# Slabs 4 and 5 of the gate/linear product over all units of an item, slabs 6 and 7 unit by unit

## The chip, the cores and the metric

The kernel runs on one core of a Trainium2 chip. The metric is the device time of one execution in microseconds (us), the median of several timed runs. The profile is one further execution recorded by the hardware profiler; its times are in microseconds from the start of the span.

## What is computed

One layer of a transformer with a recurrent group and a spatial gating group, followed by a mixture of experts. Only the last part matters here:

```python
def moe(h, router_w, router_b, w_gu, b_gu, w_down, b_down):
    logits = (hf @ router_w) + router_b              # 1024 tokens, 32 experts
    top_logit, top_e = lax.top_k(logits, TOP_K)      # TOP_K = 4
    ...
    def expert_block(args):
        xb, e = args
        gu = xb @ w_gu[e] + b_gu[e]                  # 1024 -> 2048, f32
        g, lin = jnp.split(gu, 2, axis=-1)
        g = jnp.minimum(g, SWIGLU_LIMIT)
        lin = jnp.clip(lin, -SWIGLU_LIMIT, SWIGLU_LIMIT)
        act = g * jax.nn.sigmoid(SWIGLU_ALPHA * g) * (lin + 1.0)
        return act @ w_down[e] + b_down[e]           # 1024 -> 1024
    ...                                              # times the gate, added per token
```

Everything is in f32. The 4096 assignments of tokens to experts are unevenly spread, so the experts have different numbers of rows.

## The kernel before

**Items and units.** The rows of an expert are cut into units of 32 rows, and up to four units form an item. This input gives 47 items. Item 0 is started by code of its own; the other 46 are worked off by the loop at the end of TensorE's program, `with pe.Fori(0, last_item) as g`. Of these 46, two have one unit, eleven have two, seventeen have three and sixteen have four. An expert with more than four units takes two items one after the other, on the same weights.

**TensorE.** One pass of the loop does `down_of(g)` for item g, that is a small product that makes the list of rows of a later item (`make_list`, L1430), the down product of each unit (`down`, L1499) and another small product (`repeat_rows`, L1442). Then comes `gate_and_linear_of(g + 1)`: the gate/linear product of the next item (L1479). That product is summed over eight slabs of weights, k = 0 to 7. A slab is 1 MB. For one unit and one slab TensorE issues four products of 512 columns, each split in two in the trace (eight records), into the PSUM bank of that unit. I call this a **step**: an item with n units has 8n steps. Slabs 0 to 3 are done slab by slab, each over all units. After a wait on `z_made[1]` slabs 4 to 7 are done unit by unit: four steps of the last unit, then four of the unit before it, down to unit 0. `units_down` runs a body over the units 3, 2, 1, 0, as many as the item has; it is a nest of compare-and-branch instructions (L451). `load_word` (L1463) loads two words of the next item into registers, between the last unit's products.

**Signals.** After the last slab of a unit TensorE raises `gu_made`, for which VectorE waits before it begins that unit's activation. After the product of unit 0 with slab k it raises `freed[k]` (k up to 5), so that the weights of the next expert may overwrite the slab; slabs 6 and 7 are freed in `make_list`, the four chunks of down weights during `down(0)` and `repeat_rows`. Before `down(u)` TensorE waits for `at_made`, the activated and transposed unit u.

**VectorE.** Its loop first prepares later items (L2131, L2119, L1990 to L2006), then runs `activate(u)` for the units in falling order: bias for gate and linear part (L2157, L2159), two clips (L2163, L2165), a wait for ScalarE's sigmoid (L1040), two products (L2168, L2170), and the transpose (L2172), whose end raises `at_made`. After all units come `read_list` and the result of each unit (L2179, L2182). In the last item the activation is followed by the final norm of the eight tiles of the hidden rows (L2281, L2283), into which the last results are mixed.

**Weights.** SyncE's queue issues twelve 1 MB loads for each expert, in the order of the slabs: eight of gate/linear weights (chunks 0 to 7) and four of down weights (8 to 11). Each waits for its own `freed[q]` and is issued behind the ones before it. There is one buffer for each chunk.

Of the kernel before, what the change touches and what calls it, by code (L numbers as in the profile page):

```python
# [176 lines left out]
def build(nc, ins, out):  # L177
# [10 lines left out]
    with ExitStack() as ctx:  # L188
# [260 lines left out]
        def by_units(eng, units, u, body):  # L449

            with eng.If_lt(units, u + 1):  # L451
                eng.nop()
            with eng.Else():
                body()
                eng.nop()

        def units_down(eng, units, body):

            def from_2():
                by_units(eng, units, 3, lambda: body(3))  # L460
                body(2)

            def from_1():
                by_units(eng, units, 2, from_2)
                body(1)

            by_units(eng, units, 1, from_1)
            body(0)
# [25 lines left out]
        def gu_slab(k):  # L494

            at = (k % 2) * 2048
            return big[:, SLOT_OF_PAIR[k // 2], at:at + 2048]
# [611 lines left out]
        def _(pe):  # L1109
# [339 lines left out]
            units = pe.alloc_register("units")  # L1449
# [12 lines left out]
            def load_word(turn, i):  # L1462
                pe.reg_load(loaded[i], items_i[0:1, bass.ds(turn + (IT_PLACE, IT_UNITS)[i] * WORD, 1)])  # L1463
# [7 lines left out]
            def gate_and_linear(u, half, first=False, between=None, steady=False, slabs=None):  # L1471

                for k in slabs or range(4 * half, 4 * half + 4):
                    pe.wait_ge(w_arrived[k], SEMW if first else arrived)
                    rhs = gu_slab(k).rearrange("p (a n) -> p a n", a=2)
                    if k == 0 and u > 0 and steady:
                        pe.wait_ge(dn_drained, results_of[u])
                    for j in range(4):
                        last = pe.matmul(psum[32 * j:32 * j + 32, u, :].rearrange("p (a n) -> p a n", a=2),  # L1479
                                         izT[:, k, u * UNIT:(u + 1) * UNIT], rhs[:, :, 256 * j:256 * j + 256],  # L1480
                                         start=(k == 0), stop=(k == KT - 1), skip_group_check=True)
                    if u == 0 and k < KT - 2 and not first:
                        last.then_inc(freed[k], 1)
                    if between is not None:
                        between(k % 4)
                if half == 1 and not first:
                    last.then_inc(gu_made, 1)
# [92 lines left out]
            def gate_and_linear_of(g):  # L1580

                pe.wait_ge(z_made[0], g + 1)
                for k in range(4):
                    units_down(pe, units, lambda u: gate_and_linear(u, 0, steady=True, slabs=(k,)))
                pe.wait_ge(z_made[1], g + 1)
                units_down(pe, units, lambda u: gate_and_linear(
                    u, 1, between=lambda k: load_word(g + 1, k) if k < 2 and u == 0 else None))

            def down_of(g):

# [4 lines left out]
            with pe.Fori(0, last_item) as g:  # L1595
                down_of(g)
                begin_item()
                results_to_wait_for()
                gate_and_linear_of(g + 1)
# [730 lines left out]
```

## Time and profile before

| | us |
|---|---|
| median of 3 timed runs | 2007.19 (2005.55 to 2008.69) |
| the profiled execution, its own time | 1994.71 |
| its span | 1992.9 |
| TensorE busy | 1921.6 (96%) |
| VectorE busy | 991.6 (50%) |
| mean busy share of the DMA engines' bandwidth | 262 GB/s over the span |

The loop over the items runs from about 465 us to the end. The profile's page groups instructions by line, the timeline gives them in order of time, with the idle time of the engine just before them and what ended it in brackets, and the chain names what the end of the span was waiting for, step by step. TensorE's records of one product appear as two rows of four.

### The profile page before, as it was taken

Reading aid. Unit: us, or ns where it says so; the run is one execution under the profiler, and the core shown is the slowest. Engines: PE = TensorE matmul, PEld = TensorE weight load, DVE = VectorE, ACT = ScalarE, POOL = GpSimd, SP = SyncE. Lnnn points to the kernel's source line nnn. Section 1 sums busy time; section 2 is a strip of 40 time slices with the busy share of each in tenths; the row PEclk is TensorE's granted clock in tenths of the full one; section 3 lists DMA queues with packets and bytes.
Section 4 is the critical chain, followed back from the end, with each engine's and each line's share of the span. In section 5 each row is a group of like instructions: output and inputs, shape, how many; then the busy total and the mean of one; then the engine's idle time right before and its main releaser. Section 6 shows DMA issues by size and latency. Waiting matters only on the chain.

```text
span 1992.9 us, 54916 instructions
## 1 busy us (share of the span) xinstructions
PE 1921.6 (96%) x20484; PEld 805.8 (40%) x20485; DVE 991.6 (50%) x2305; ACT 357.8 (18%) x739; POOL 461.6 (23%) x498
## 2 busy tenths in 40 slices
PE   7999999969899899999999999999999999999996
PEld 4444445424333334343434343333443444344432
DVE  2677565255444444544445444554545454454435
ACT  4353122221111111101111111111111111111003
POOL 1200041033222222122222222222222223222221
PEclk9999999989999999999999999999999999999998
DMA  9433326153843946869595978979889797999985
GB/s 349 162 116 127 127 108 204 69 190 106 338 161 105 350 132 230 338 203 371 173 370 207 386 262 307 384 281 386 292 341 351 279 395 286 389 398 343 328 329 201
DMA packets 120672, 521.86 MB, mean 262 GB/s; under 512 B 14592, under 2 KB 40848, under 8 KB 71472
## 3 DMA queue, kind: packets, MB, share of 16 engines
q1 hardware_dynamic: 88880, 468.41, 60.5%
q0 software_dynamic: 31168, 50.78, 11.0%
q10 hardware_dynamic: 576, 2.10, 0.3%
q8 instruction: 21, 0.34, 0.1%
q14 instruction: 27, 0.22, 0.0%
HBM read 488.85 MB, written 32.78 MB: 262 GB/s over the span
## 4 chain that ended last, share of the span: by engine, by line
PE 91%; DMA 4%; DVE 2%; issue 1%; SPq 1%; DVEq 1%; ACT 0%; POOL 0%; POOLq 0%; ACTq 0%
PE psum L1479 46%; PE psum L1499 24%; PE psum L1153 7%; PE psum L1386 5%; PE psum L1321 3%; DMA big<-in_exp_w_down_dram 3%; PE psum L1220 1%; DMA big<-in_ada_w_dram 1%; PE psum L1254 1%; PE psum L1430 1%; PE psum L1442 0%; DMA big<-in_w_out_dram 0%; PE psum L1314 0%; PE psum L1339 0%; DVEq L444 0%
## 5 line engine op out<-in xcount | busy, mean ns | idle before, releaser
L1479 PE MATMUL psum<-big,r 128*32 128x512 f32 x9152 | 995.8, 594 | 8.2 <-ACT r L1045 4.7
L1479 PEld LDWEIGHTS psum<-big,r 128*32 128x32 f32 x9152 | 292.2, 110 | 665.9 <-issue 656.3
L1499 PE MATMUL psum<-big,r 128*32 128x256 f32 x9152 | 508.7, 382 | 13.0 <-DVE r L2172 9.8
L1499 PEld LDWEIGHTS psum<-big,r 128*32 128x32 f32 x9152 | 295.5, 111 | 205.5 <-DVE r L2172 9.9
L783 POOL DMA_INDIRECT acc_rows<-r,scatter_idx x139 | 221.4, 1593 | 676.3 <-DVE r L2182 617.0
L1030 ACT ACTIVATE r<-r,shift 128x128 f32<-128x128 f32 x368 | 150.9, 481 | 839.5 <-PE psum L1479 798.3
L2179 DVE TENSOR_TENSOR r<-psum,r 128x256 f32<-128x256 f32 x143 | 60.7, 424 | 267.5 <-PE psum L1499 266.5
L2157 DVE TENSOR_TENSOR r<-psum,r 128x256 f32<-128x256 f32 x143 | 60.4, 423 | 251.8 <-PE psum L1479 233.9
L2131 DVE STREAM_TRANSPOSE r<-r 128x1024 f32<-128x1024 f32 x46 | 95.9, 2084 | 170.8 <-issue 170.8
L772 POOL DMA_INDIRECT r<-hs_rows,gather_idx x143 | 142.4, 996 | 123.5 <-issue 123.5
L1040 ACT ACTIVATE r<-r 128x256 f32<-128x256 f32 x143 | 59.6, 417 | 473.9 <-DVE r L2163 473.9
L1153 PE MATMUL psum<-r,big 128*128 128x512 f32 x320 | 139.0, 593 | 0.0
L1386 PE MATMUL psum<-big,r 128*128 128x512 f32 x256 | 112.1, 594 | 1.0 <-DMA big<-in_w_out_dram 1.0
L2172 DVE STREAM_TRANSPOSE r<-r 128x256 f32<-128x256 f32 x143 | 93.6, 654 | 4.9
L1153 PEld LDWEIGHTS psum<-r,big 128*128 128x128 f32 x320 | 60.6, 190 | 75.1 <-issue 75.1
L2168 DVE TENSOR_TENSOR r<-r 128x256 f32<-128x256 f32 x143 | 60.9, 426 | 49.7 <-ACT r L1040 49.7
L762 POOL COPY gather_idx<-r 128x4 int32 (+1 forms) x47 | 8.8, 188 | 316.1 <-DVE r L1999 316.1
L2182 DVE SCALAR_TENSOR_TENSOR r<-r,g1row,g_rows 128x256 f32<-128x256 f32 x143 | 69.3, 485 | 5.1
L1386 PEld LDWEIGHTS psum<-big,r 128*128 128x128 f32 x256 | 47.9, 190 | 59.2 <-issue 57.3
L2119 DVE TENSOR_TENSOR r<-r 128x1024 bf16<-128x1024 f32 (+1 forms) x49 | 60.0, 1225 | 7.1 <-DVE r L2117 1.2
L2170 DVE TENSOR_TENSOR r<-r 128x256 f32<-128x256 f32 x143 | 60.8, 425 | 4.9
L2159 DVE SCALAR_TENSOR_TENSOR r<-psum,r 128x256 f32<-128x256 f32 x143 | 59.2, 414 | 0.1
(326 smaller groups left out, 983.5 us busy)
## 6 DMA issues: line engine op xcount, KB each, us to landing
big<-in_exp_w_gu_dram SPq DMA_DIRECT2D x256, 1024.0 KB, 10.0
big<-in_exp_w_down_dram SPq DMA_DIRECT2D x128, 1024.0 KB, 17.0
big<-in_ada_w_dram SPq DMA_DIRECT2D x8, 2048.0 KB, 13.0
r<-bias_pack SPq DMA_DIRECT2D x128, 96.0 KB
big<-in_ada_w_dram SPq DMA_DIRECT2D x8, 1024.0 KB, 12.6
big<-in_w_in_dram SPq DMA_DIRECT2D x4, 2048.0 KB, 17.3
r<-in_x_dram SPq DMA_DIRECT2D x12, 512.0 KB, 10.2
big<-in_w_out_dram SPq DMA_DIRECT2D x2, 2048.0 KB, 12.8
```

Source lines behind the costliest of these rows:

```text
L772: pool.indirect_dma_start(z_quarters[:, u, :], None, hs_quarters, bass.IndirectOffsetOnAxis(ap=gather_idx[:, u:u + 1], axis=0)).then_inc(r ...
L783: pool.indirect_dma_start(acc_quarters, bass.IndirectOffsetOnAxis(ap=scatter_idx[:, u:u + 1], axis=0), y_sb[:, u, :], None, bounds_check=4 ...
L1030: ins_ = act.activation(izT[:, k, :].rearrange("p (u n) -> p u n", u=UMAX), z_blocks[:, :, k, :], ACT.Identity, bias=shift2[:, 1, k:k + 1] ...
L1153: last = pe.matmul(b, w[:, k, m * P:(m + 1) * P], zT[:, k, th * 512:(th + 1) * 512], start=(k == 0), stop=(k == KT - 1))
L1386: last = pe.matmul(b, src[:, ct % CT, t * P:(t + 1) * P], ring(("wout", dh))[:, ct, :], start=(ct == 0), stop=(ct == 2 * CT - 1))
L1479: last = pe.matmul(psum[32 * j:32 * j + 32, u, :].rearrange("p (a n) -> p a n", a=2), izT[:, k, u * UNIT:(u + 1) * UNIT], rhs[:, :, 256 * ...
L1499: ins_ = pe.matmul(psum[32 * i:32 * i + 32, DOWN_BANK[u], 0:256], actT[:, u, f, :], down_slab(f)[:, 256 * i:256 * i + 256], start=(f == 0) ...
L2131: dve.transpose(z_blocks, z_quarters.rearrange("p u (n k) -> p u k n", k=KT)).then_inc(z_blocked, 1)
L2168: dve.tensor_tensor(gsig_sb[:, u % 2, :], gate_u, sig_sb[:, u % 2, :], ALU.mult).then_inc(gsig_made, 1)
L2170: dve.tensor_tensor(act_sb[:, u % 2, :], lin_u, gsig_sb[:, u % 2, :], ALU.mult).then_inc(act_made, 1)
L2172: dve.transpose(actT[:, u, :, :], act_sb[:, u % 2, :].rearrange("p (n k) -> p k n", k=KT)).then_inc(at_made, 1)
L2182: dve.scalar_tensor_tensor(out=y_sb[:, u, :], in0=y_sb[:, u, :], scalar=gate_cur[:, u:u + 1], in1=g2_rows[:, :], op0=ALU.mult, op1=ALU.mul ...
```

## The change

The loop over slabs that serves slabs 0 to 3 is repeated for slabs 4 and 5, after the wait on `z_made[1]`: slab 4 over all units of the item, then slab 5 over all units. Only slabs 6 and 7 are left to the unit-by-unit form. `load_word` moves from behind slabs 4 and 5 of unit 0 to behind slabs 6 and 7 of unit 0. Item 0, which has its own code, is unchanged. No product, transfer or signal is added or taken away.

```diff
                 for k in range(4):
                     units_down(pe, units, lambda u: gate_and_linear(u, 0, steady=True, slabs=(k,)))
                 pe.wait_ge(z_made[1], g + 1)
+                for k in (4, 5):
+                    units_down(pe, units, lambda u: gate_and_linear(u, 0, steady=True, slabs=(k,)))
                 units_down(pe, units, lambda u: gate_and_linear(
-                    u, 1, between=lambda k: load_word(g + 1, k) if k < 2 and u == 0 else None))
+                    u, 1, slabs=(6, 7), between=lambda k: load_word(g + 1, k - 2) if u == 0 else None))
```

The instructions of TensorE at two places follow, before and after. `w_arrived4` is the arrival of slab 4 (chunk 4), and so on. The first place is the start of the second half of the product, where before the first unit gets its four slabs in a row:

```order
L451 COMPARE_AND_BRANCH
L451 UNCONDITIONAL_BRANCH
L1479 MATMUL psum<-big,r 32x512 [waits w_arrived4]
L1479 MATMUL psum<-big,r 32x512 x3
L1479 MATMUL psum<-big,r 32x512 [waits w_arrived5]
L1479 MATMUL psum<-big,r 32x512 x3
L1479 MATMUL psum<-big,r 32x512 [waits w_arrived6]
L1479 MATMUL psum<-big,r 32x512 x3
L1479 MATMUL psum<-big,r 32x512 [waits w_arrived7]
L1479 MATMUL psum<-big,r 32x512 x3
L453 UNCONDITIONAL_BRANCH
```

After the change the same unit gets slabs 6 and 7 in a row, behind the branches that close slab 5 of unit 0:

```order
L1479 MATMUL psum<-big,r 32x512 [waits w_arrived5]
L1479 MATMUL psum<-big,r 32x512 x3
L451 COMPARE_AND_BRANCH
L451 UNCONDITIONAL_BRANCH
L451 COMPARE_AND_BRANCH
L451 UNCONDITIONAL_BRANCH
L451 COMPARE_AND_BRANCH
L451 UNCONDITIONAL_BRANCH
L1479 MATMUL psum<-big,r 32x512 [waits w_arrived6]
L1479 MATMUL psum<-big,r 32x512 x3
L1479 MATMUL psum<-big,r 32x512 [waits w_arrived7]
L1479 MATMUL psum<-big,r 32x512 x3
```

Slabs 4 and 5 of that unit have moved ahead of it, and those of all other units with them. The second place is the end of the product for unit 0 on TensorE, with the words of the next item. Before:

```order
L1463 ISA
L1463 TENSOR_LOAD r
L1479 MATMUL psum<-big,r 32x512 x4
L1463 ISA
L1463 TENSOR_LOAD r
L1479 MATMUL psum<-big,r 32x512 x8
L1595 ISA
L1595 COMPARE_AND_BRANCH
```

After:

```order
L1463 ISA
L1463 TENSOR_LOAD r
L1479 MATMUL psum<-big,r 32x512 x4
L1463 ISA
L1463 TENSOR_LOAD r
L1597 ISA
L1597 COMPARE_AND_BRANCH
```

The two loads have moved two steps later, the second of them to the loop's own branch.

## Rows read from the trace of the kernel before

**Rows 1.** The page: span, and the two product groups (xcount, busy, mean, idle)
```profile
span 1992.9 us, 54916 instructions
...
L1479 PE MATMUL psum<-big,r 128*32 128x512 f32 x9152 | 995.8, 594 | 8.2 <-ACT r L1045 4.7
...
L1499 PE MATMUL psum<-big,r 128*32 128x256 f32 x9152 | 508.7, 382 | 13.0 <-DVE r L2172 9.8
```

**Rows 2.** Timeline of TensorE, a two-unit item (start, duration, instructions)
```profile
1003.87 13.94 PE L1479 MATMUL psum<-big,r 128*32 128x512 f32 x128
...
1018.02 7.11 PE L1499 MATMUL psum<-big,r 128*32 128x256 f32 x128
...
1025.26 1.07 PE L1479 MATMUL psum<-big,r 128*32 128x512 f32 x8
```

**Rows 3.** Timeline of VectorE in the same two-unit item
```profile
1014.86 0.42 DVE L2157 TENSOR_TENSOR r<-psum,r 128x256 f32<-128x256 f32 x1 [1.02 <-PE psum L1479]
...
1017.30 0.65 DVE L2172 STREAM_TRANSPOSE r<-r 128x256 f32<-128x256 f32 x1
...
1018.05 0.42 DVE L2157 TENSOR_TENSOR r<-psum,r 128x256 f32<-128x256 f32 x1
...
1020.48 0.66 DVE L2172 STREAM_TRANSPOSE r<-r 128x256 f32<-128x256 f32 x1
```

**Rows 4.** Timeline, a four-unit item: product, and start of its first activation
```profile
961.84 27.67 PE L1479 MATMUL psum<-big,r 128*32 128x512 f32 x256
...
979.47 0.42 DVE L2157 TENSOR_TENSOR r<-psum,r 128x256 f32<-128x256 f32 x1 [7.90 <-PE psum L1479]
```

**Rows 5.** Timeline, a three-unit item: gate/linear product, its down product
```profile
1067.28 20.81 PE L1479 MATMUL psum<-big,r 128*32 128x512 f32 x192
...
1088.31 10.57 PE L1499 MATMUL psum<-big,r 128*32 128x256 f32 x192
```

**Rows 6.** Timeline of TensorE: first and last of the eleven two-unit items
```profile
792.88 13.94 PE L1479 MATMUL psum<-big,r 128*32 128x512 f32 x128
...
1667.79 13.94 PE L1479 MATMUL psum<-big,r 128*32 128x512 f32 x128
```

**Rows 7.** Timeline of TensorE: the two items that wait for weights
```profile
1135.13 7.93 PE L1479 MATMUL psum<-big,r 128*32 128x512 f32 x72 [1.64 <-DMA big<-in_exp_w_gu_dram]
...
1147.14 7.98 PE L1499 MATMUL psum<-big,r 128*32 128x256 f32 x144 [1.06 <-DMA big<-in_exp_w_down_dram]
...
1223.23 7.93 PE L1479 MATMUL psum<-big,r 128*32 128x512 f32 x72 [1.81 <-DMA big<-in_exp_w_gu_dram]
...
1235.66 7.98 PE L1499 MATMUL psum<-big,r 128*32 128x256 f32 x144 [1.39 <-DMA big<-in_exp_w_down_dram]
```

**Rows 8.** Windows: busy PE, PEld, DVE, ACT, POOL; granted clock, DMA share, GB/s
```profile
1084.00:1086.00 2.00, 2.00 (x24) 0.65 (x20) 1.72 (x5) 0.11 (x1) 0.00 (x0) 1.00 0.01 4
1088.00:1096.00 8.00, 8.00 (x156) 4.95 (x156) 4.08 (x12) 1.96 (x5) 1.47 (x1) 1.00 1.01 425
1100.00:1133.00 33.00, 33.00 (x384) 11.93 (x373) 16.18 (x41) 5.67 (x14) 9.02 (x10) 1.00 1.03 400
```

**Rows 9.** Timeline of TensorE, a one-unit item, and a window on its down product
```profile
681.13 6.19 PE L1499 MATMUL psum<-big,r 128*32 128x256 f32 x64 [4.86 <-DVE r L2172]
...
681.10:687.30 6.20, 6.17 (x66) 2.82 (x67) 0.10 (x2) 0.00 (x0) 1.81 (x3) 0.58 1.02 419
```

**Rows 10.** Timeline of the last item: its gate/linear product, then VectorE
```profile
1931.04 27.67 PE L1479 MATMUL psum<-big,r 128*32 128x512 f32 x256
...
1958.95 0.42 DVE L2157 TENSOR_TENSOR r<-psum,r 128x256 f32<-128x256 f32 x1 [0.35 <-PE psum L1479]
...
1963.14 0.16 DVE L2281 RECIPROCAL rstd<-srt 128x1 f32<-128x1 f32 x1 [1.10 <-ACT srt L1081]
...
1981.09 0.53 DVE L2296 SCALAR_TENSOR_TENSOR r<-r 128x256 f32<-128x256 f32 x1
```

**Rows 11.** TensorE's sequencer at the line of `load_word`: durations in ns
```profile
L1463 PEldq TENSOR_LOAD <-r x95: 295/304/491, 438.9 to 1954.4; - x95
```

## The prediction

> **What bounds the kernel now.** I began with the page's busy shares and its two product groups: TensorE works in 96% of the span, and the gate/linear and down products are 1504 us of it [rows 1]. So a change in the loop over items costs time only where it makes TensorE wait, or behind TensorE's last product. Then I read TensorE's timeline through the loop, item by item, for gaps in front of the down product. Two units take 13.94 us, three 20.81 and four 27.67 [rows 2, 4, 5]: 6.87 us a unit, 0.859 us a step, with no gap between slabs in either half. The first down product starts 14.15 us after the start of a two-unit item (1018.02 - 1003.87) and 21.03 us after that of a three-unit item (1088.31 - 1067.28) [rows 2, 5], at once behind the little list product.
>
> What comes close to holding it is the activation. In the two-unit item VectorE starts unit 1 at 10.99 us after the item's start and ends its transpose at 14.08 (1017.95); TensorE's down product follows 0.07 us later [rows 2, 3]. So there the cover is already used up to the last 0.1 us. An activation takes 3.09 us from first instruction to transposed, and two in a row start 3.19 us apart (1014.86, 1018.05) [rows 3].
>
> **The change part by part.** (1) **The first unit is complete later.** With n units, before, the last unit has all slabs after 4n + 4 steps; after the change after 6n + 2 (slabs 0 to 5 over n units, then two steps). The later units follow every two steps instead of every four; unit 0 ends at 8n as before. How long after completion the activation starts is shown by the four-unit item: 20 steps are 17.18 us, the activation starts at 17.63 (979.47 - 961.84) [rows 4], so 0.45 us later.
>
> Two units: complete after 14 steps, 12.03 us; start 12.48; transposed 15.57; down product at 15.64 instead of 14.15. **TensorE waits 1.49 us.** Before, unit 1 was complete after 12 steps, 10.31 us, and VectorE began at 10.99, later than completion asks (10.76), for its own preparations ended then; these are over by 12.48, so only completion counts. Unit 0 is then activated from 15.67 to 18.76, and its down product is due 15.64 + 3.48 = 19.12 (a unit of down work is half of 7.11 less the overlap [rows 2]): no second wait. All that follows on TensorE, the next item above all, moves by 1.49.
>
> Three units: complete after 20 steps, 17.18; start 17.63; ready 20.79 with the 0.07; TensorE comes at 21.03 [rows 5]. Hidden, with 0.24 us to spare; unit 1 is ready at 23.98 against 24.5, unit 0 at 27.2 against 28.0. If the cover were gone by 0.1 us at each, seventeen items would cost 1.7. Four units: complete after 26 steps, 22.33; ready 25.9 against 27.9, and one unit every 3.19 after that against 3.48 of down work. Hidden. One unit: the order of its eight steps is unchanged, and so is its wait [rows 9].
>
> There are eleven two-unit items [rows 6]. Two of them stand right in front of the two items that wait for weights, so I count nine here: 9 x 1.49 = **+13.4 us**.
>
> (2) **The end of the kernel.** The last item has four units. Before, its last activation starts at 1958.95, 0.44 us after TensorE's last gate/linear step, and from there VectorE and ScalarE run in one line to the last instruction at 1981.09, with one idle time of 1.10 for ScalarE's root [rows 10]. TensorE's down product ends within that. After the change units 3 to 0 queue on VectorE: unit 3 starts at 1931.04 + 22.33 + 0.45 = 1953.82, unit 0 three intervals of 3.19 later, 1963.39. The final norm stands behind it in the same queues, so all of it shifts: **+4.4 us**. With an interval of 3.0 it would be 3.9; if the down product hid it, zero.
>
> (3) **Weights are needed later and freed earlier.** Slab 7 is first used after 6n + 1 steps instead of 4n + 3, in a three-unit item 19 instead of 15: 3.4 us of grace. Slab 4 is freed after 5n steps instead of 8n - 3, slab 5 after 6n instead of 8n - 2: 2.6 and 1.7 us earlier with two units, 5.2 and 3.4 with three. This helps where weights are late. Only two items show such waits, both with three units behind a two-unit item: 1.64 + 1.06 = 2.70 us and 1.81 + 1.39 = 3.20 [rows 7]. The waits for slab 7 (1.64, 1.81) go, but then the same queue is met at the down weights: chunk 11 lands when the transfers before it are done, and from 1088 to 1133 they run at 425 and 400 GB/s without a hole [rows 8]. A slab freed earlier inside a full queue lands nothing sooner. The only hole that the earlier release can use is that at 1084 to 1086, 4 GB/s [rows 8], one item before. Two transfers pulled forward across it leave that much less work waiting later, but at 1096 the four down chunks are not free yet, so most of it is lost again. I take 0.5 us for each of the two places. The bounds are nothing, and all that remains of the waits when the 1.49 in front of them is taken off, 1.21 and 1.71, in sum 2.9. The stall of these two two-unit items disappears in the wait behind it. Together **-1.0 us**.
>
> (4) **Branches and register loads.** Two further `units_down` put some compare-and-branch pairs on TensorE's sequencer for each item; the same pairs stand between slabs 0 to 3, where the four-unit product loses nothing [rows 4]. A register load takes 0.304 us of the sequencer [rows 11]; two of them now stand nearer to the loop's branch. The sequencer runs ahead of the array, and they cost nothing where they stand now. Nought, with an upper bound of 46 x 0.3 = 14 us if the second load lay bare at the end of each item; what speaks against it is that the loop's own branch shows no gap there either: the list product follows on the last step.
>
> (5) **What is queued behind.** VectorE's results of the first units in four- and three-unit items start up to 4 us later, behind the activations; that of unit 0 comes last as before, and with it the end of VectorE's pass, so GpSimd's scatters and the next preparations don't move. ScalarE's scaling of the next item's second half waits behind the sigmoids, some 4 us later in a four-unit item, with the whole down product and four slabs before it is needed. Zero.
>
> Sum: 13.4 + 4.4 - 1.0 = +16.8 us. On the profiled execution 1994.71 + 16.8 = 2011.5; on the median, 12.5 us above that execution, 2007.19 + 16.8 = **2024.0**.
>
> **The rivals.** *Faster, by weights.* The timed runs are 12.5 us longer than the profiled one; I don't know in what. If it were late weights, at the eleven items behind a two-unit item, the stall there would vanish into them and the later need of slab 7 would pay. Place: the first slabs 4 to 7 behind each two-unit item. At a wait of 3.4 us each, all removable, the gain is 11 x (3.4 - 1.49) = 21.1, less the 4.4 at the end: 2007.2 - 16.7 = 1990.5. It decides from a mean wait of 1.49 + (4.4 + 4.0)/11 = 2.25 us upward. Against it: nine of the eleven show no such wait, and 9 x 2.25 = 20 us is more than the whole difference of 12.5. 4%.
>
> *No change.* The stall is covered after all, or late weights swallow it in the timed runs as they do at two items in the profile, and the last norm hides in the down product: 2007 plus or minus 4. For it speaks only that I infer completion from counted steps. 6%.
>
> *The clock falls.* After the wait of 4.86 us in a one-unit item the granted clock is 0.58 on average (half, 1.2 GHz, for most of it), and 64 records of down product take 6.19 us where two units take 7.11, that is 3.5 for one [rows 2, 9]: 2.7 us lost. If each 1.49 us wait did that, 11 x 2.7 = 29.7 more: 2054. Against it: after waits of 1.64 and 1.81 us the 72 records, nine steps, take 7.93 us, the full 2.4 GHz pace [rows 2, 7]. [...] 5%.
>
> *The loads lie bare.* Up to 14 us on top: about 2031 to 2038. 4%.
>
> *Only half of it.* The interval of activations or the shift of the end is smaller than I read, or weights give back all 2.9: 2012 to 2019. 11%.
>
> **How the numbers follow.** The forecast itself, 2019 to 2030, has 70%; its ends are the sum with 1.2 us a stall, 3.9 at the end and 2.9 of weights given back (10.8 + 3.9 - 2.9 = 11.8), and with 1.7 us a stall, 1.7 for the three-unit items and nothing back (15.3 + 4.4 + 1.7 = 21.4), with 1.5 us of spread of the runs. Range 2013 to 2031; it takes in the half case and leaves out the clock, the faster one, most of no change and of the bare loads. A measurement of this kernel can tell about 0.2%, 4 us, from no change. Faster by more than that 4%, within it 7%, slower 89%.
>
> **What would show it.** In the changed profile the two-unit items have a wait of about 1.5 us in front of the first L1499, released by VectorE's L2172, and last 22.9 us instead of 21.4. Three- and four-unit items last as long as before. The waits for gate/linear weights are gone, those for down weights at the two places are larger than 1.06 and 1.39. The last activation begins some 5 us after TensorE's last gate/linear step instead of 0.44. Wrong would be: no wait at L1499 (then completion isn't what starts the activation), waits in three-unit items (the 0.24 us was no cover), a granted clock under 1 in two-unit items, or a gap ahead of L1430 (the loads lie bare).

## The result, and the profile after

| | median, us | runs |
|---|---|---|
| before | 2007.19 (2005.55 to 2010.05) | 11 |
| after the change | 2012.42 (2010.46 to 2013.90) | 11 |

The ratio is 1.0021, 95% interval 1.0012 to 1.0029: 5.2 us slower, at the edge of what can be told from no change. I had forecast 16.8 us, 2024.0 with a range from 2013; the measured time lies just below the range. The sign is right, the forecast size is three times too large.

And yet the profile of the changed kernel is 2012.2 us long, against 1992.9 before [rows 1]: 19.3 more. The two profiled executions differ by about what I had forecast; the medians don't. In part that is chance: of the 19.3 us, 1.7 lie ahead of the loop, where nothing was changed, and the two-unit items of this trace are longer by 18.2 together, of which the stall that I forecast makes 15.8; the rest are the second interruptions shown at the end of this section. So the question of this study is not where 17 us come from, but why 12 of them are missing in the first comparison.

The page of the changed kernel, span and the two product groups:

```profile
span 2012.2 us, 55222 instructions
...
L1479 PE MATMUL psum<-big,r 128*32 128x512 f32 x9152 | 994.2, 593 | 6.0 <-ACT r L1045 5.8
...
L1499 PE MATMUL psum<-big,r 128*32 128x256 f32 x9152 | 511.2, 383 | 28.2 <-DVE r L2174 14.1
```

The idle time in front of L1499 has grown from 13.0 to 28.2 us. The page puts 14.1 of it down to VectorE; most of the rest stands in the trace as `<-issue`, though it has the same place and the same 1.37 us. (VectorE's and later lines stand two further down in the new file: L2174 is the old L2172, L2159 the old L2157.) TensorE and VectorE in a two-unit item, to be laid beside [rows 2, 3]; in brackets the idle time just before:

```profile
1106.60 13.94 PE L1479 MATMUL psum<-big,r 128*32 128x512 f32 x128
1120.48 0.35 PE L1430 MATMUL psum<-g1row,r 128*128 128x6 bf16 x8
1122.20 7.11 PE L1499 MATMUL psum<-big,r 128*32 128x256 f32 x128 [1.37 <-DVE r L2174]
1129.25 0.25 PE L1442 MATMUL psum<-g1row,r 128*128 128x6 bf16 x4
1129.43 1.06 PE L1479 MATMUL psum<-big,r 128*32 128x512 f32 x8
```
```profile
1119.08 0.42 DVE L2159 TENSOR_TENSOR r<-psum,r 128x256 f32<-128x256 f32 x1 [2.45 <-PE psum L1479]
...
1121.51 0.64 DVE L2174 STREAM_TRANSPOSE r<-r 128x256 f32<-128x256 f32 x1
1122.07 0.38 DVE L2159 TENSOR_TENSOR r<-psum,r 128x256 f32<-128x256 f32 x1
```

The activation starts 12.48 us after the item (forecast 12.48), the down product at 15.60 (forecast 15.64), and the item lasts 22.83 us. Two activations now follow each other by 2.99 us, not 3.19. In the three-unit items nothing moved: L1499 still comes 21.03 us after L1479, here 0.3 us after the transpose for it ends:

```profile
1074.89 20.81 PE L1479 MATMUL psum<-big,r 128*32 128x512 f32 x192
1095.63 0.36 PE L1430 MATMUL psum<-g1row,r 128*128 128x6 bf16 x8
1095.92 0.42 PE L1499 MATMUL psum<-big,r 128*32 128x256 f32 x4
```
```profile
1092.53 0.42 DVE L2159 TENSOR_TENSOR r<-psum,r 128x256 f32<-128x256 f32 x1 [7.45 <-PE psum L1479]
...
1094.96 0.66 DVE L2174 STREAM_TRANSPOSE r<-r 128x256 f32<-128x256 f32 x1
```

Of the waits for weights [rows 7] the two at the gate/linear product are gone; at the down product one of 1.23 us is left at the second place. I had forecast both down waits to grow beyond 1.06 and 1.39; neither did:

```profile
1216.03 20.81 PE L1479 MATMUL psum<-big,r 128*32 128x512 f32 x192
...
1241.09 7.98 PE L1499 MATMUL psum<-big,r 128*32 128x256 f32 x144 [1.23 <-DMA big<-in_exp_w_down_dram]
```

The last item begins at 1946.53 and the span ends 65.7 us later, before 61.9: the end has grown by 3.8 us. Its last activation on VectorE, to be laid beside [rows 10], starts 4.2 us after TensorE's last gate/linear step:

```profile
1978.24 0.39 DVE L2159 TENSOR_TENSOR r<-psum,r 128x256 f32<-128x256 f32 x1
...
1982.39 0.16 DVE L2283 RECIPROCAL rstd<-srt 128x1 f32<-128x1 f32 x1 [1.10 <-ACT srt L1081]
```

One thing I had not foreseen. In three two-unit items the down product is interrupted a second time, at about its thirtieth record, by nothing that the profile can name:

```profile
794.45 13.94 PE L1479 MATMUL psum<-big,r 128*32 128x512 f32 x128
808.32 0.36 PE L1430 MATMUL psum<-g1row,r 128*128 128x6 bf16 x8
810.04 1.93 PE L1499 MATMUL psum<-big,r 128*32 128x256 f32 x31 [1.36 <-issue]
812.32 5.56 PE L1499 MATMUL psum<-big,r 128*32 128x256 f32 x97 [0.35 <-issue]
```

### The profile page after: what moved, and what is told of

It reads as the page before. It is cut to its first block, busy times and chain, and to the rows that moved or that the text cites. A ratio compares the mean times of both kernels' runs of the same rounds, so it can differ in the third digit from the quotient of the medians.

```text
span 2012.2 us, 55222 instructions
## 1 busy us (share of the span) xinstructions
PE 1926.1 (96%) x20484; PEld 823.3 (41%) x20485; DVE 977.7 (49%) x2305; ACT 357.9 (18%) x739; POOL 461.0 (23%) x498
## 4 chain that ended last, share of the span: by engine, by line
PE 89%; DMA 4%; DVE 3%; issue 2%; DVEq 1%; SPq 1%; ACT 1%; POOL 0%; ACTq 0%; POOLq 0%
PE psum L1479 45%; PE psum L1499 24%; PE psum L1153 7%; PE psum L1386 5%; PE psum L1321 3%; DMA big<-in_exp_w_down_dram 2%; PE psum L1220 1%; DMA big<-in_ada_w_dram 1%; PE psum L1254 1%; PE psum L1430 1%; PE psum L1442 0%; DMA big<-in_w_out_dram 0%; PE psum L1314 0%; PE psum L1339 0%; DVEq L444 0%
## 5 line engine op out<-in xcount | busy, mean ns | idle before, releaser
L1479 PE MATMUL psum<-big,r 128*32 128x512 f32 x9152 | 994.2, 593 | 6.0 <-ACT r L1045 5.8
L1479 PEld LDWEIGHTS psum<-big,r 128*32 128x32 f32 x9152 | 299.7, 110 | 654.9 <-issue 649.8
L1499 PE MATMUL psum<-big,r 128*32 128x256 f32 x9152 | 511.2, 383 | 28.2 <-DVE r L2174 14.1
L1499 PEld LDWEIGHTS psum<-big,r 128*32 128x32 f32 x9152 | 304.2, 111 | 215.3 <-issue 21.2
L2159 DVE TENSOR_TENSOR r<-psum,r 128x256 f32<-128x256 f32 x143 | 56.6, 396 | 373.6 <-PE psum L1479 371.9
L2174 DVE STREAM_TRANSPOSE r<-r 128x256 f32<-128x256 f32 x143 | 93.4, 653 | 4.9
L2172 DVE TENSOR_TENSOR r<-r 128x256 f32<-128x256 f32 x143 | 60.8, 425 | 4.9
```

The lines of the kernel that those rows point to most:

```text
L1499: ins_ = pe.matmul(psum[32 * i:32 * i + 32, DOWN_BANK[u], 0:256], actT[:, u, f, :], down_slab(f)[:, 256 * i:256 * i + 256], start=(f == 0) ...
L2172: dve.tensor_tensor(act_sb[:, u % 2, :], lin_u, gsig_sb[:, u % 2, :], ALU.mult).then_inc(act_made, 1)
L2174: dve.transpose(actT[:, u, :, :], act_sb[:, u % 2, :].rearrange("p (n k) -> p k n", k=KT)).then_inc(at_made, 1)
```

## The experiments

### Is the profiled execution of before one of its usual ones?

e1, e4, e10 and e16 are the kernel before without any edit, on four different chips. On record are five chips: one for e1 and e2, one for e3 and e4, one for e5, e7, e8 and e9, one for e6 and e10 to e12, one for e13 to e16. The chip of the first comparison is not on record.

> The kernel before, unchanged, profiled once more. The one profiled execution of before took 1994.7 us where its timed runs lie at 2005.6 to 2010.1; that of the changed kernel took 2013.9, inside its timed runs of 2010.5 to 2013.9. Theory A (the profiled execution of before was an exception, and its usual executions lose some 12.5 us that the changed kernel does not lose): this profile is 2005 to 2010 us long, and the items' own lengths show where the 12.5 us are, as waits for weights (A1), at half clock in some stretch (A2), or ahead of the loop (A3). Theory B (profiling itself makes this kernel quicker than its timed runs): the profile is again near 1995 us, with the timed runs near 2007.

Measured: 1993.7 us (1991.6 to 1999.0) with a profile of 1990.3; the kernel before beside it 1994.4. Neither A nor B: on this chip all executions take 1994 us. By their times, the rows of before come from a chip of this kind, the first comparison from one on which before takes 2007. So I had added the sum of one chip to the median of another.

> The kernel before, one more profile, for the case that this is a chip where it takes about 2007 us: then the items' own lengths show where 12.5 us are lost. If it is weights that come later there, items of three units behind items of two wait by more than 3.2 us, or items beside them wait too; if it is the clock, single items are longer at a granted clock below 1; if neither, it lies ahead of the loop or behind it. If the chip is one where before takes about 1994 us, it repeats the profile of before within 2 us.

> The kernel before, one profile, for the case that this is a chip where it takes about 2007 us: then gaps in TensorE's records show where 12.5 us are lost. In the changed kernel's first trace, taken beside the runs of 2007, TensorE's sequencer three times got no instructions for 0.7 to 1.0 us in a two-unit item's down product. If that is what before suffers from, it shows some dozen such gaps. On a chip where before takes 1994 us it repeats the profile of before within 2 us and shows none.

Two further chips with before at 1994.6 and 1994.0 (profiles of 1990.9 and 1992.2 us). No gap, no other wait than in [rows 7, 9].

### Does the forecast hold where the profile holds?

e3 is the whole change once more, on one of these chips.

> The whole change again, beside the kernel before on one and the same chip. On the chip of the last two runs the kernel before takes 1994.4 us (as its profile said), not 2007.2. Theory 1 (the sum of the profile is right, and the first timed comparison was made on a chip on which the kernel before loses 12.5 us more): where before takes about 1994, the changed kernel takes 1994.4 + 2.7 (the large items alone, measured) + 11 x 1.43 = about 2011, ratio 1.008. Theory 2 (the profile's sum does not carry over to timed runs): ratio near 1.002, about 1999. Should this run fall on a chip where before takes about 2007, theory 1 expects 2012 again.

Measured: 2009.26 against 1994.57, ratio 1.0077 (1.0063 to 1.0091), +14.7 us. Theory 1 holds. From the traces of e3 and e4: the eleven two-unit items are longer by 1.44 each and once by 1.6 (15.9 together), the end by 3.8, the waits for weights are shorter by 4.7 (6.1 to 1.4), in sum +15.0. The two spans differ by 15.9; the other 0.9 lies ahead of the loop, where nothing was changed.

e2 leaves small items as they were:

```diff
+                with pe.If_lt(units, 3):
+                    ...                      # slabs 4 to 7 unit by unit, as before
+                with pe.Else():
+                    ...                      # slabs 4 and 5 over all units, then 6 and 7
```

> The change for items of three and four units only; items of one and two units keep the old order, by one branch for each item. The eleven waits of 1.43 us in front of the two-unit items' down products go. Theory 1 (the arithmetic of the profile holds for timed runs too, and something of 12.5 us that before loses is absent with the new order of large items): 2012.4 - 11 x 1.43 + up to 3 for the two items behind which weights are late = about 1997 to 2000. Theory 2 (what before loses in its timed runs hangs on the two-unit items, whose down product comes within 0.1 us of the activation, and the change removed it by making the stall whole): the loss comes back, 2007 + 3.8 at the end = about 2011. Theory 3 (it is in late weights): between them, 2001 to 2006.

Measured: 1997.11 beside 1994.36, ratio 1.0014 (1.0004 to 1.0023), +2.75. Without the new order in the two-unit items 12 us of the loss are gone: theory 1. The profiled execution of e2 took 1999.69 us, 2.6 above its median, so its trace shows more loss than its usual run has. It shows something beside theory 1, at the first place with late weights. Before, the wait is split (e1, same chip):

```profile
1133.49 7.93 PE L1479 MATMUL psum<-big,r 128*32 128x512 f32 x72 [1.21 <-DMA big<-in_exp_w_gu_dram]
...
1145.39 7.98 PE L1499 MATMUL psum<-big,r 128*32 128x256 f32 x144 [0.96 <-DMA big<-in_exp_w_down_dram]
```

In e2 it stands at the down product alone:

```profile
1119.82 20.81 PE L1479 MATMUL psum<-big,r 128*32 128x512 f32 x192
...
1143.80 1.07 PE L1499 MATMUL psum<-big,r 128*32 128x256 f32 x16 [1.02 <-DMA big<-in_exp_w_down_dram]
1146.24 9.66 PE L1499 MATMUL psum<-big,r 128*32 128x256 f32 x144 [1.37 <-DMA big<-in_exp_w_down_dram]
```

The same 144 records take 9.66 us instead of 7.98. The window on them (busy PE, PEld, DVE, ACT, POOL; granted clock; DMA) shows why:

```profile
1146.00:1149.00 3.00, 2.76 (x28) 1.45 (x32) 1.33 (x5) 0.30 (x1) 0.00 (x0) 0.58 0.00 0
```

After two waits with 1.07 us of work between them the granted clock is 0.58 on average, half for most of the window. The item lasts 36.2 us, 4.5 more than without late weights, in e1 2.6. At the second place of e2 waits of 0.66 and 1.40 us went before the same fall. But e5, which has the same order in these items, kept the granted clock at 1 with waits as long as these:

```profile
1233.79 1.07 PE L1499 MATMUL psum<-big,r 128*32 128x256 f32 x16 [0.83 <-DMA big<-in_exp_w_down_dram]
1236.24 7.98 PE L1499 MATMUL psum<-big,r 128*32 128x256 f32 x144 [1.38 <-DMA big<-in_exp_w_down_dram]
```

So the length of the two waits alone doesn't decide whether the clock falls, and no run shows what does. The waits themselves hardly shrank by the new order: 2.2 and 2.3 us at the two places in e1, 2.4 and 2.1 in e2, 1.6 and 2.2 in e5. A later need of gate/linear weights with late down weights behind it gains little by itself.

### The parts one by one

e7 is e2 turned round: the new order in items of one and two units, the old one in the others. e6 has it in the last item alone (the last pass of the loop is written out behind it). e5 has small items and the last item in the old order. e9 puts only slab 4 over all units; e8 moves only the register loads:

```diff
-                for k in (4, 5):                     # e9, against the change
+                for k in (4,):
...
-                    u, 1, between=lambda k: load_word(g + 1, k) if k < 2 and u == 0 else None))      # e8, against before
+                    u, 1, between=lambda k: load_word(g + 1, k - 2) if k >= 2 and u == 0 else None))
```

> The new order for items of one and two units only, large items in the old one. Theory 1: eleven waits of 1.43 us in front of the two-unit items' down products; two of them are taken back by shorter waits for weights behind them, so 9 x 1.43 = 12.9 us above before on a chip where before takes 1994 us; no shift of the end. Rival (the stall is hidden in timed runs): within 4 us of before. On a chip where before takes 2007 us this kernel, with the large items in the old order, tells whether what is lost there goes with the small items (then about 2010) or with the large ones (then about 2020).

> The old order in the loop, the new one in the last item alone. Theory 1: the last four activations queue on VectorE, the last one starts 3.8 us later and the final norm stands behind it: 3.8 us above before (an interval of 2.97 us between activations, not 3.19), about 1998.3 where before takes 1994.5. Rival (the end is hidden in the down product, or e5's gain over e2 came from elsewhere): within 1 us of before.

> As e2 (items of three and four units in the new order, smaller ones in the old), and the last item in the old order too. Theory 1: e2's loss of 2.7 us is the 3.8 us shift of the end, plus 1.4 + 0.4 at the two items behind which weights are late, less what is not named; with the end restored it is the same as before or up to 1.5 us above, and its activations end 0.4 + 3.1 us after TensorE's last gate/linear step. Rival: the loss of e2 is not at the end (branches, or the longer activation queue in four-unit items); then this one stays 2.7 us above before.

> A smaller dose: only slab 4 over all units, slabs 5 to 7 unit by unit. In a two-unit item unit 1 is complete after 13 steps (11.17 us) instead of 12 or 14, the activation starts at 11.62 and the down product at 14.74 instead of 14.16: a wait of 0.58 us, 9 x 0.58 = 5.2. At the end the last unit's activation starts 1.3 us later. Theory 1: 6.5 us above before, less up to 1 for weights. Rival (the loss is a step of its own, for any change of order): as large as the whole change's 14.7.

> The old order of slabs, only load_word behind slabs 6 and 7 of unit 0 instead of 4 and 5. Theory 1: no difference to before (within 1 us). Rival (the loads lie bare at the end of each item): up to 46 x 0.3 = 14 us above before, with a gap in front of L1430. On a chip where before takes 2007 us its trace also shows where the 12.5 us are, since nothing else differs from before.

| kernel | median, us | before beside it | ratio (95%) | difference | expected |
|---|---|---|---|---|---|
| e7 | 2007.96 | 1994.60 | 1.0071 (1.0054 to 1.0088) | +13.4 | +12.9 |
| e6 | 1997.22 | 1993.99 | 1.0017 (1.0007 to 1.0026) | +3.2 | +3.8 |
| e5 | 1993.79 | 1994.60 | 1.0000 (0.9991 to 1.0010) | -0.8 | 0 to +1.5 |
| e9 | 2001.66 | 1994.60 | 1.0044 (1.0032 to 1.0057) | +7.1 | +6.5 |
| e8 | 1994.09 | 1994.60 | 0.9999 (0.9989 to 1.0008) | -0.5 | 0 |

The ratio isn't the quotient of the two medians, so it agrees with the difference only to 1 or 2 us; its interval reaches 2 to 3 us to each side. Each term of theory 1 shows alone, and the stall at a smaller dose too: in e7's trace all eleven two-unit items last 22.83 us, in e9's all eleven last 21.97, that is 0.58 more than 21.39, the figure expected. The stall and the shift of the end are the whole loss on these chips; branches and register loads cost nothing that an interval of 2 us would show. e5 avoids both losses and is no faster than before: where few weights come late the new order has nothing to give.

### What is lost on the chip of the first comparison?

Two ideas were left: weights that come later there, or TensorE's sequencer (which hands the engine its instructions) running dry, as in the three items above. e11 and e12 test the first by force, before and the change with more to transfer:

```diff
                     load_chunk(e, q)
+                    if q in (3, 5):
+                        sp_.dma_start(extra_rows[place - 1, q // 5], chunk_source(e, 0)).then_inc(param_in, SEMW)
```

> The kernel before, with two further transfers of 1 MB for each expert (weights copied to an unused place in device memory) in the queue behind chunks 3 and 5, so that weights come later. Nothing computed changes. It is compared with e12. Theory L (on the chip of the first comparison weights come later, and this alone makes before lose 12.5 us and the change 3): here before loses clearly more than the changed kernel, by 5 us or more. Theory 1: both orders end up waiting for chunk 11, so a later queue costs both nearly the same; each extra transfer moves the landing at the two places by 2.6 to 5 us, together +10 to +20, and the difference between the kernels stays near 14.7 or shrinks by at most 3.

> The changed kernel with the same two further transfers. Theory L: it loses 3 us where e11 loses 12, so that it stands 5 us or less above e11. Theory 1: it stands 11 to 15 us above e11.

Measured: before 2137.25 (+143), the change 2099.45 (+105 over before without extra traffic, 90 over the change in e3, on another chip), with 1993.99 beside them. My theory 1 was wrong here: the two did not keep their distance; the order of the two turned round by more than 50 us. The list of waits (engine, line, released by; sum, times, longest), first of e11, then of e12:

```profile
PE psum L1483 <- DMA big<-in_exp_w_gu_dram: 90.9, 33, 5.7
...
PE psum L1503 <- DMA big<-in_exp_w_down_dram: 7.3, 6, 1.4
```
```profile
PE psum L1483 <- DMA big<-in_exp_w_gu_dram: 35.7, 17, 3.7
PE psum L1503 <- DVE r L2178: 24.8, 13, 4.9
PE psum L1503 <- DMA big<-in_exp_w_down_dram: 21.3, 21, 1.4
```

Waits for gate/linear weights fall from 90.9 to 35.7 us, 14 come back at the down product and 15 as stalls. The clock takes part: between 480 and 1960 us it was at half for 130 us in e11 and for 61 in e12, against 14 in e10. The gain is mostly in places that wait in neither kernel without the extra traffic: a four-unit item behind a small one is up to 9.8 us longer in e11 and 0 to 4.2 in e12. So the new order is worth much once weights are late in many items. Whether the later need of slabs 4 to 7 does it or the earlier release of slabs 4 and 5, no run separates. e13 to e15 ask whether a little of this makes the first comparison. e13 is before, e14 the change and e15 the kernel e5, each with a quarter of the extra traffic:

```diff
+                    if q == 5:                                           # 0.5 MB instead of 2
+                        sp_.dma_start(extra_rows[place - 1], chunk_source(e, 0)[:, 0:1024]).then_inc(param_in, SEMW)
```

> The kernel before with one further transfer of 0.5 MB for each expert, behind chunk 5 in the weights' queue: a quarter of e11's extra traffic. In e11 the two transfers of 1 MB cost some items 8 to 14 us, about 6 us for each MB. Theory L (a small lateness costs before much and the change little): 3 us later at each place; the two items behind 2-unit items of two-unit experts wait 3 us more each, and five to six three-unit items begin to wait by 1 to 3 us: 10 to 16 us above before, 2004 to 2010. Rival (the order turns round only when the queue is overloaded): under 6 us, 2000 or less.

> The changed kernel with the same 0.5 MB. Theory L: its later need of slabs 4 to 7 covers the three-unit items; only the two places behind two-unit experts wait longer, by 1.5 to 3 us each: 3 to 6 us above the change, 2012 to 2015, so that it stands 3 to 8 us above e13, near the 5 us of the first comparison. Rival: it stands 12 us or more above e13.

> e5 (small items and the last item in the old order, large items in the new one) with the same 0.5 MB. Theory L: it has the later need of weights without the stall of 1.43 us in eleven items and without the 3.8 us at the end: 1998 to 2001, below both e13 and e14. Rival (the gain of the new order under late weights comes from the stalls in two-unit items, which give the queue time): about as e13.

> The kernel before, one profile, for the case that this is a chip where it takes about 2007 us. Theory L expects there waits for gate/linear weights of 1 to 3 us in several three-unit items, 12.5 us in sum above the 5.9 us of before; the sequencer theory expects gaps without a wait. On a chip where before takes 1994 us it repeats the profile of before within 2 us.

They ran on a chip of the other kind: the kernel before beside them takes 2008.84 us (2007.95 to 2011.2). e13 takes 2022.43 (ratio 1.0066, 1.0049 to 1.0083), e14 2023.68 (1.0072, 1.0055 to 1.0088), e15 2019.89 (1.0051, 1.0034 to 1.0068). The absolute figures of the expectations are missed, since the base is another. Against its own base e13's +13.6 is within the 10 to 16 of theory L (weights that come a little later make before lose much and the change little), but e14 stands 1.3 us above e13 and not 3 to 8, and e15 is 2.5 below e13 and not 3 to 12. Theory L is settled by e16, the trace of before on this chip, 2008.26 us: its waits for weights make 3.2 us in the loop, against 4.2 in e10, and it has the pauses without any wait that the sequencer theory of e10 and e16 expected. A two-unit item on it:

```profile
1334.42 13.94 PE L1479 MATMUL psum<-big,r 128*32 128x512 f32 x128
1348.30 0.35 PE L1430 MATMUL psum<-g1row,r 128*128 128x6 bf16 x8
1348.82 2.02 PE L1499 MATMUL psum<-big,r 128*32 128x256 f32 x29 [0.16 <-DVE r L2172]
1351.16 5.84 PE L1499 MATMUL psum<-big,r 128*32 128x256 f32 x99 [0.33 <-issue]
1356.93 0.25 PE L1442 MATMUL psum<-g1row,r 128*128 128x6 bf16 x4
```

and the same item of the same kernel on e1's chip:

```profile
1325.85 13.94 PE L1479 MATMUL psum<-big,r 128*32 128x512 f32 x128
...
1340.01 7.11 PE L1499 MATMUL psum<-big,r 128*32 128x256 f32 x128
1347.06 0.25 PE L1442 MATMUL psum<-g1row,r 128*128 128x6 bf16 x4
```

The down product starts 14.40 us after the item instead of 14.16, then TensorE breaks off after 29 records of the first unit's down product and goes on late; the item lasts 22.69 us instead of 21.39. For the break no semaphore and no transfer is named. The weight loads show it from the sequencer's side:

```profile
1351.20 5.32 PEld L1499 LDWEIGHTS psum<-big,r 128*32 128x32 f32 x98 [0.63 <-issue]
```

The weight loads pause as well, with nothing in the profile that holds them, so the engine seems to have had no next instruction. In another item there are two such breaks:

```profile
806.63 2.72 PE L1499 MATMUL psum<-big,r 128*32 128x256 f32 x29
809.70 0.38 PE L1499 MATMUL psum<-big,r 128*32 128x256 f32 x1 [0.35 <-issue]
810.49 5.77 PE L1499 MATMUL psum<-big,r 128*32 128x256 f32 x98 [0.41 <-issue]
```

Summed over e16's items against [rows 2, 5]: the eleven two-unit items are longer by 0.3 to 2.6 us each, 16.6 together; no item of three or four units is longer but by weights (and by 0.2 us once). The waits for weights are 2.5 less than in the first profile, since these breaks stand in front of them. That makes 16.6 - 2.5 = +14.1, and the spans differ by 13.6. So all that this chip loses, it loses in the two-unit items. The traces of e13 and e15, both with the old order in small items on the same chip, show the same: their eleven two-unit items are longer by 18.0 and 17.8 together.

The changed kernel stalls in the same items, 1.43 us just before the place of the break. In its first trace, which belongs to the runs of 2012, the two-unit items are longer by 18.3 us together: 1.44 in seven of them, where no break is left, and 1.5 to 2.5 in the four others. Before 16.6, after 18.3: the stall costs 1.7 us there, where it costs 15.9 on the other chips. e14 shows it on e16's own chip: the new order's two-unit items are longer by 19.0, that is 1.0 and 1.2 more than in e13 and e15; seven of them last 22.83 us, and the four longer ones are the same four as in the first trace of the change.

With the end (+3.8) and the weights (4.3 to 1.8, -2.5) the sum for the first trace of the change against e16 is +3.0. The spans of the two differ by 5.7: the loop starts 2.0 us later in the changed one, and small remainders make 0.7. That later start is not the change's, since e10, a trace of before, has it as well (480.9 us against 478.8 in e4). How often it occurs in the timed runs isn't known. So the terms of the change give 3.0 of the 5.2 us between the medians, and whether the other 2 are this start is open; the runs of either kernel spread by 3.4 to 4.5 us.

What stays open: why the sequencer runs dry. It comes about 4 us behind the branches that jump over the products of units 3 and 2, in two-unit items and on some chips only, so that instructions fetched too late are likely; no run took the fetch by itself, and I call it argued, not shown. Nor does any run show why chips differ in it. That the first comparison ran on a chip like e16's is inferred from the time of before (2007.2 and 2008.8) and from the first trace of the change, which e14 repeats item by item.

## Why the prediction was wrong

- **Part 1, the stall.** Right as a mechanism and to 0.04 us in place: 15.60 against 15.64, confirmed by e7 and at a smaller dose by e9. (That e7's +13.4 equals the forecast +13.4 is partly luck: eleven stalls of 1.44 less the weights gained.) Wrong as a term of the sum on the median: on a chip like that of the comparison it is worth 1.0 to 1.7 us instead of the forecast 13.4, because the same items of before already lose 16.6 us there by something that a stall hides. One reading of [rows 3] was wrong without touching the sum: unit 1's activation did not wait for VectorE's own preparations. Its row names TensorE's L1479 after 1.02 us of idle time; why it came 0.23 us later than the counted steps ask isn't shown.
- **How the sum was carried over.** This is the step that failed: "on the median, 12.5 us above that execution". It took for granted that the unknown 12.5 us and the 13.4 us of part 1 add up; they lie in the same items, and there before loses 16.6 us and the changed kernel 18.3. I saw that the profiled execution lay outside the timed runs, named it as unknown, tried it against late weights only, gave that 4%, and added the two numbers all the same. With this gap unexplained the range should have reached down to the case that the gap and the stall lie at the same place: 2007.2 + 4.4 - 1.0 = 2010.6. The measured 2012.42 lies within the rival "Only half of it" (2012 to 2019), but its reasons (smaller terms) make only 1.8 of the 11.6 us that are missing, as the 15.0 of the traces of e3 and e4 against 16.8 shows.
- **Part 2, the end.** 4.4 forecast, 3.8 in the trace, 3.2 by e6. Activations follow each other by 2.97 to 2.99 us when nothing else is on VectorE; my 3.19 was from a pair whose second activation could start only when its own unit was complete: 16 steps, 13.74 us, and 0.45 give 14.19 after the item's start, and it came at 14.18 [rows 2, 3]. The row at 1981.09 that I called the last instruction isn't: the span runs to 1992.9 [rows 1]. Both ends shift alike, so the sum stands.
- **Part 3, weights.** I took two of eleven stalls as absorbed and 1.0 besides, 4.0 in all; e3 against e4 gives 4.7. The sign that I named for it, down waits above 1.06 and 1.39 us, did not come: they shrank. And "a slab freed earlier inside a full queue lands nothing sooner" holds for these two places only. e11 and e12 show the new order worth over 50 us when weights are late in many items; the rival "faster, by weights" was a real mechanism with the wrong condition.
- **Part 4, branches and loads.** Nought, as said (e8 for the loads, e5 for the branches).
- **Part 5.** Three- and four-unit items last as long as before on all chips but for 0.1 to 0.3 us in a few, as said.
- **The clock** did not fall at a stall of 1.4 us. It fell in e2, where two waits stand close together, and not at a like pair in e5.

## What to carry to other kernels

If the profiled execution lies outside the timed runs, the difference has a place in the program; before a forecast is put on the median, ask for each term whether that difference could lie in the same place and hide it. Summing slabs over all units before finishing any of them completes the first unit later and needs the last slabs' weights later by the same steps. Here it paid only where weights were what TensorE waited for in many items, and cost where the consumer of the first unit was already just in time. A wait is best judged by who would be ready next: here the activation had at most 0.07 us of cover before the change in two-unit items, and 0.3 us left after it in three-unit ones, and the cost followed from that to a few hundredths of a microsecond.

## What the runs showed of the hardware

- The same kernel takes 1994 us on four chips, and 2007 to 2009 on one further chip and in the first comparison, each with a spread of 3 to 8 us. On the one such chip whose trace is at hand the difference is not spread over the program: it is in pauses of TensorE of up to 1.1 us that neither a semaphore nor a transfer explains, at one kind of item (e16: 16.6 us in eleven two-unit items; e1, e4, e10: none).
- Such a pause is gone where a wait of 1.4 us stands just ahead of it, in seven items of eleven (the first trace of the change, and e14 again).
- One wait of 1.4 us in an item, or 1.64 and 1.06 with 11 us between them, left the granted clock at 1. Two of 1.02 and 1.37 us, or of 0.66 and 1.40, with 1.07 us of work between them were followed by half clock for some 3 us and 144 records 1.7 us longer (e2); two of 0.83 and 1.38 were not (e5).
